# A third place for modulation weights, and the entry of the rotary attention in another order

## The reference, cut to what matters

```python
# first block, layer 1: keys and values from the norm with norm_kv, queries from norm_mix[1]
kv = _rmsnorm(h, norm_kv) @ w_kv
ks_ = _rope(ks_.reshape(b, s, N_HEADS, HEAD_DIM))
q = _rope((hn @ w_q_b[j]).reshape(b, s, N_HEADS, HEAD_DIM))
# _rope: [a1 * cos - a2 * sin, a2 * cos + a1 * sin]
...
# second block: w_ada_2 is 1024 x 6144
mod = jax.nn.silu(c) @ w_ada[l] + b_ada[l]
sh1, sc1, g1, sh2, sc2, g2 = jnp.split(mod[:, None, :], N_MOD, axis=-1)
u = rmsnorm(h, norm1_w[l]) * (1.0 + sc1) + sh1
```

## Time and profile before

| what | value |
|---|---|
| time, median of 3 runs | 1903.96 us (1902.36 to 1904.41) |
| the profiled execution's own time | 1905.59 us |
| its span in the trace | 1903.7 us |
| TensorE busy, granted clock over the span | 1854.5 us (97%), 0.993 |
| VectorE, ScalarE, GpSimd busy | 1302.0, 1036.9, 228.8 us |
| `down0` and the entry behind it | about 506 to 664 us of the span |
| `down1` | about 1111 to 1248 us of the span |

### The profile page before, as it was taken

The page is one execution under the profiler, slowest core; times in us unless marked ns, Lnnn a source line. Parts: engine busy times, 40 slices in busy tenths (PEclk is TensorE's granted clock), DMA queues, the critical chain, the costliest instruction groups (busy, mean ns, idle before and its releaser), DMA issues.

```text
span 1903.7 us, 29122 instructions
## 1 busy us (share of the span) xinstructions
PE 1854.5 (97%) x10924; PEld 1597.7 (84%) x10924; DVE 1302.0 (68%) x1962; ACT 1036.9 (54%) x1838; POOL 228.8 (12%) x239
## 2 busy tenths in 40 slices
PE   7999999999999899999999999999999999999997
PEld 6778788999888677778999987778888779999886
DVE  5566657888666767755888856598667687777322
ACT  5556545555577544445555557665556455555322
POOL 0000020111111100001111102211111101111000
PEclk9999999999999899999999999999999999999999
DMA  4211135666565322224566655532221135666431
GB/s 141 67 66 62 38 110 150 161 153 153 177 204 194 133 89 88 88 66 143 144 151 161 159 185 182 182 106 77 73 72 56 56 128 149 166 148 152 148 98 64
DMA packets 82452, 235.29 MB, mean 124 GB/s; under 512 B 10017, under 2 KB 10529, under 8 KB 81569
## 3 DMA queue, kind: packets, MB, share of 16 engines
q1 hardware_dynamic: 57984, 176.06, 27.9%
q0 software_dynamic: 23248, 56.11, 13.6%
q10 hardware_dynamic: 1104, 1.58, 0.2%
HBM read 221.12 MB, written 8.39 MB: 121 GB/s over the span
## 4 chain that ended last, share of the span: by engine, by line
PE 54%; DVE 5%; ACT 4%; DMA 3%; issue 2%; SPq 0%; POOL 0%; DVEq 0%; ACTq 0%; POOLq 0%
PE ps L413 9%; PE ps L415 9%; PE ps L414 9%; PE ps L1030 6%; PE ps L1031 6%; PE ps L1032 6%; PE ps L2825 2%; DMA wada<-in_ada 1%; PE ps L1636 1%; DMA tmps<-in_ada 1%; DVE wlo L395 1%; PE ps L1661 1%; PE ps L1651 1%; ACT wada L1488 1%; ACT tmps L1488 1%
## 5 line engine op out<-in xcount | busy, mean ns | idle before, releaser
L395 DVE TENSOR_TENSOR wlo<-raw,whi 128x1024 fp32r<-128x1024 f32 (+1 forms) x188 | 238.1, 1271 | 108.3 <-ACT whi L384 108.2
L413 PE MATMUL ps<-xh,whi 128*128 128x512 f32 x672 | 272.2, 405 | 6.3 <-DVE wlo L395 2.8
L414 PE MATMUL ps<-xl,whi 128*128 128x512 f32 x672 | 264.0, 393 | 0.0
L415 PE MATMUL ps<-xh,wlo 128*128 128x512 f32 x672 | 263.9, 393 | 0.0
L1031 PE MATMUL ps<-xl,whi 128*128 128x256 f32 x864 | 244.5, 283 | 0.0
L1030 PE MATMUL ps<-xh,whi 128*128 128x256 f32 x864 | 244.5, 283 | 0.0
L1032 PE MATMUL ps<-xh,wlo 128*128 128x256 f32 x864 | 244.4, 283 | 0.0
L384 ACT ACTIVATE whi<-raw 128x1024 fp32r<-128x1024 f32 (+1 forms) x196 | 197.9, 1023 | 76.2 <-PE ps L415 76.2
L413 PE MATMUL ps<-acth,whi 128*128 128x512 f32 x528 | 210.8, 399 | 8.8 <-DVE wlo L395 8.7
L784 ACT ACTIVATE whi<-raw 128x1024 fp32r<-128x1024 f32 x162 | 147.5, 911 | 112.5 <-PE ps L1032 99.1
L414 PE MATMUL ps<-actl,whi 128*128 128x512 f32 x528 | 206.0, 390 | 0.0
(11 more groups left out here) (382 smaller groups left out, 3770.1 us busy)
## 6 DMA issues: line engine op xcount, KB each, us to landing
raw<-in_gu SPq DMA_DIRECT2D x78, 512.0 KB, 3.8
raw<-in_down SPq DMA_DIRECT2D x48, 512.0 KB, 4.6
raw<-in_gu SPq DMA_DIRECT2D x54, 256.0 KB, 4.4
raw<-in_gu POOLq DMA_DIRECT2D x54, 256.0 KB, 4.5
raw<-in_qkv SPq DMA_DIRECT2D x24, 512.0 KB, 4.4
wada<-in_ada POOLq DMA_DIRECT2D x24, 512.0 KB, 3.8
tmps<-in_ada POOLq DMA_DIRECT2D x24, 512.0 KB, 3.9
raw<-in_qkvb SPq DMA_DIRECT2D x24, 512.0 KB, 3.8
```

What stands on the lines that cost most here:

```text
L395: eng.tensor_tensor(wlo[:, s, 0:n], raw[:, s, 0:n], whi[:, s, 0:n].bitcast(F32), ALU.subtract).then_inc(lo_done, 1)
L413: pe.matmul(ps[:, bank], whi[:, s, w], hi[:, k0 + k], start=start and k == 0, stop=False)
L414: pe.matmul(ps[:, bank], whi[:, s, w], lo[:, k0 + k], start=False, stop=False)
L415: mm = pe.matmul(ps[:, bank], wlo[:, s, w], hi[:, k0 + k], start=False, stop=stop and k == n - 1)
```

## The change

The fourth slot of `wlo` becomes a third place for units of `w_ada` in both down projections. The three places are used in turn, in an order that differs between the two phases, so that the last unit of the first phase lies in the new place, and the last in the second phase in the pair `tmps[:, 0:2]`. Three loads are issued at the start of a phase, and the load of unit n waits for the folding of unit n-3.

In the entry of the rotary attention, VectorE takes the query out of PSUM right behind the norm (ahead of the last four `yl`), splits the value unit directly behind the last `yl`, then takes the key out, splits the next query unit, multiplies both by `cosine`, and only then folds the last unit of `w_ada`. The two sign changes of `sine` go to ScalarE, behind a wait for the three tables and ahead of the two splits and two swaps that ScalarE makes there. TensorE makes the two last `ada_tile`s ahead of the last block of the value unit instead of between key and value unit. One semaphore is shared by two uses (`in_t`, `f_turned`) to make room for the third landing semaphore. Nothing else of the other stages changes.

```diff
+        third = top[0] + 3 * UNIT * 4
         wlo = place("wlo", [P, 4, UNIT], F32R)
...
-        ada_w = [wada[:, :], tmps[:, 0:2].rearrange("p a b -> p (a b)")]
+        ada_third = place("ada_third", [P, UNIT], F32, third)
+        ada_pair = tmps[:, 0:2].rearrange("p a b -> p (a b)")
+        ada_w = [(ada_pair, wada[:, :], ada_third[:, :]), (ada_third[:, :], wada[:, :], ada_pair)]
...
-                    wait(pool, ada_sum, n - 1)
-                    pool.dma_start(ada_w[n % 2], a["ada"][n, :, :]).then_inc(ada_in[n % 2], 16)
+                    wait(pool, ada_sum, n - 2)
+                    pool.dma_start(ada_w[n // 24][n % 3], a["ada"][n, :, :]).then_inc(ada_in[n % 3], 16)
...
-                load_ada(0, 2)
+                load_ada(0, 3)
...
-                    load_ada(3 * m + 2, 3 * m + 5)
+                    load_ada(3 * m + 3, 3 * m + 6)
...
-            par = j % 2
-            act.wait_ge(ada_in[par], t * 48 + 16 * ((24 * half + j) // 2 + 1))
+            par = j % 3
+            act.wait_ge(ada_in[par], t * 32 + 16 * ((24 * half + j) // 3 + 1))
...
                     split_hi(act, U["qkvb"], (0, 2))
+            act.wait_ge(at1.loaded, 48)
+            for part in (0, 64):
+                act.activation(sine[part:part + 32, :], sine[part:part + 32, :], ACT.Copy, scale=-1.0).then_inc(at1.signed, 1)
             u = U["qkvb"]
...
+            def query_first():
+
+                dve.wait_ge(mm_done, U["qkvb"].number(0, 0) + 1)
+                dve.scalar_tensor_tensor(tmp[0][:, :], ps[:, 6], 0.125, rstd[:, :], ALU.mult, ALU.mult)\
+                   .then_inc(at1.out, 1)
...
                 if m == 3:
                     refine_rest(dve, r0f)
-            ada_product(dve, 0, 3, 5)
-            dve.wait_ge(ada_sum, 24)
-            wait(dve, r0f.rstd, 4)
+                    wait(dve, r0f.rstd, 4)
+                    query_first()
+            split_lo(dve, U["qkvb"], (0, 2))
...
+            def rope_g(t):
                 if leading(t):
+                    key_out(t)
+                    split_lo(dve, u, ahead(u, t, 1, False))
+                    dve.wait_ge(at1.loaded, 48)
+                    query_cosined(t)
+                    key_cosined(t)
+                    ada_product(dve, 0, 3, 5)
+                    turn(t, 0, qrot)
                     ada_evac(dve, 0)
...
-                        if leading(t):
-                            for part_of in (4, 5):
-                                ada_tile(pe, 0, 3, part_of)
                     else:
                         pe.wait_ge(at1.out, 3 * t + 1)
-                        product(pe, u, t, 2, 6, yh, yl)
+                        product(pe, u, t, 2, 6, yh, yl, late=last_columns if leading(t) else None)
```

More of the change, by code:

```diff
@@ L442, in build @@
         e_lo = fast_prod = sem("e_lo_fast_prod")
-        in_t = sem("in_t")
+        in_t = sem("in_t_f_turned")
         out_in = sem("out_in")
-        f_ready, f_turned, f_moved = sem("f_ready"), sem("f_turned"), sem("f_moved")
+        f_ready, f_moved = sem("f_ready"), sem("f_moved")
+        f_turned = Since(in_t, KT)
         f_late, f_early = sem("f_late"), sem("f_early")
@@ L1118, in build @@
         hn = HeadNorm()
-        ada_in = [sem(f"ada_in{i}") for i in range(2)]
+        ada_in = [sem(f"ada_in{i}") for i in range(3)]
         ada_scaled = sem("ada_scaled")
@@ L1482, in ada_scale @@
         def ada_scale(act, half, t, j):
-            par = j % 2
-            act.wait_ge(ada_in[par], t * 48 + 16 * ((24 * half + j) // 2 + 1))
+            par = j % 3
+            act.wait_ge(ada_in[par], t * 32 + 16 * ((24 * half + j) // 3 + 1))
             for k in range(KT):
-                w = ada_w[par][:, k * P:(k + 1) * P]
+                w = ada_w[half][par][:, k * P:(k + 1) * P]
                 last = act.activation(w, w, ACT.Copy, scale=csil[:, k:k + 1])
@@ L1491, in ada_product @@
         def ada_product(dve, half, t, j):
-            n, par = t * 6 + (24 * half + j), j % 2
-            w = ada_w[par]
+            n = t * 6 + (24 * half + j)
+            w = ada_w[half][j % 3]
             dve.wait_ge(ada_scaled, n + 1)
@@ L2147, in _ @@
                     if m == 4:
-                        act.wait_ge(f_turned, 4)
+                        wait(act, f_turned, 4)
                         for b in range(NB):
@@ L2285, in turn, with query_cosined @@
                 dve.tensor_tensor(dst[:, :], dst[:, :], tmp[3 + i][:, :], ALU.add).then_inc(at1.roped, 1)
[L2287 to L2293, removed]
-                if leading(t):
[L2295 to L2300, removed]
+            def query_cosined(t):
@@ L2301, in rope_g, with key_out, key_cosined @@
                 dve.wait_ge(at1.out, 3 * t + 1)
                 dve.tensor_tensor(tmp[3][:, :], tmp[0][:, :], cosine, ALU.mult).then_inc(at1.cosined, 1)
-                split_lo(dve, u, ahead(u, t, 1, False))
+            def key_out(t):
                 dve.wait_ge(mm_done, u.number(t, 1) + 1)
                 dve.tensor_tensor(tmp[1][:, :], ps[:, 7], rstd[:, :], ALU.mult).then_inc(at1.out, 1)
+            def key_cosined(t):
                 dve.wait_ge(at1.out, 3 * t + 2)
                 dve.tensor_tensor(tmp[4][:, :], tmp[1][:, :], cosine, ALU.mult).then_inc(at1.cosined, 1)
+            def rope_g(t):
@@ L2308, in rope_g @@
                 if leading(t):
-                    ada_evac(dve, 0)
-                turn(t, 0, qrot)
-                if not leading(t):
+                    key_out(t)
[5 more added lines that the diff above has]
+                    turn(t, 0, qrot)
+                    ada_evac(dve, 0)
+                else:
+                    split_lo(dve, u, ahead(u, t, 0, False))
+                    dve.wait_ge(mm_done, u.number(t, 0) + 1)
+                    wait(dve, at1.roped, 2 * t)
+                    dve.scalar_tensor_tensor(tmp[0][:, :], ps[:, 6], 0.125, rstd[:, :], ALU.mult, ALU.mult)\
+                       .then_inc(at1.out, 1)
+                    query_cosined(t)
+                    split_lo(dve, u, ahead(u, t, 1, False))
+                    key_out(t)
+                    key_cosined(t)
+                    turn(t, 0, qrot)
@@ L2628, in _ @@
             wait(dve, f_rstd, 4)
-            dve.wait_ge(f_turned, KT)
+            wait(dve, f_turned, KT)
             for b in range(NB):
@@ L2737, in _, with last_columns @@
             u = U["qkvb"]
+            def last_columns():
+                for part_of in (4, 5):
+                    ada_tile(pe, 0, 3, part_of)
             def rope_g(t, part=(0, 1, 2)):
@@ L2981, in turn_rows @@
                     mm = pe.transpose(ps[:, 2 + b, m % 4 * P:(m % 4 + 1) * P], gain_h[:, m, b * P:(b + 1) * P], ident[:, :])
-                mm.then_inc(f_turned, 1)
+                mm.then_inc(f_turned.sem, 1)
             def sum_rows(squares, start):
```

1 line of the change is left out of this document (removed).

## The result

The changed kernel takes 1889.37 us, the median of 4 runs (1888.84 to 1890.44); the kernel before takes 1903.16 us, the median of 4 runs (1902.31 to 1904.41). The ratio is 0.9928, with a 95% interval of 0.9911 to 0.9945: 13.8 us shorter, within the range and next to the forecast of 1889.6. The sum behind the forecast was 14.4 us, counted from 1904.0; the fourth run of the kernel before brought its median down by 0.8 us, and so the time fits better than the gain. The profiled execution took 1888.85 us.

What follows compares the result with a forecast made beforehand. In `down1` late `w_ada` loads were taken to hold a 16.20 us round against TensorE's 15.70; 8.0 + 1.1 + 0.7 + 2.3 + 2.3 = 14.4 us off 1905.59, less 1.6 for the median, gave 1889.6 us, about 3 us either side.

Steps and rivals of the forecast that it cites:

- Part 1: Third place in `down1`: earlier loads remove TensorE's waits for low parts, 8.0 us, plus 1.1 us behind the last tile.
- Part 2: Third place in `down0`: 0.7 us within the tiles and 2.3 us at its end, ahead of the sum over partitions.
- Part 3: New order of the entry: scores start 2.3 us earlier, counted from S, the start of the sum over partitions.
- the clock's 0.94 us: Entry: with TensorE idle under 1 us before the sum over partitions, its clock stays and the norm's last step comes earlier.
- the 11.0 us from the value unit's low part to the scores: Entry: time from low part through SyncE's queue of loads and swaps to the scores, taken as 11.0 us before and after.
- rival (d): Scores: TensorE's idle time before them gets short enough for the clock to stay, 2.3 us less: 1887.3 us; chance 0.05.
- Rival (b): Entry gains nothing, key's swaps being late or TensorE waiting in the value unit: 2.3 us less gain, 1893 us; chance 0.12.
- (a): Another chain holds `down1`, tiles end at 16.4 us, half the gain there goes, 4 us: 1893.6 us; chance 0.12.
- (c): Waits put down to landings are really for SyncE's load or TensorE; only 2.3 us remain: 1901.7 us; chance 0.04.
- (e): Writes into the low parts' memory slow TensorE's reads in both down projections, 2.5 us per cent, 1910 at 8%; chance 0.02.
- six signs named: Landings, 0.75 us waits, 15.7 us tiles in `down1`; sum's wait under 1 us; value's low part at 8.4, scores 19.4 us.
- three signs of being wrong: `down1` rounds above 15.8 us without landings; sum over partitions waiting over 2 us; key's swaps landing later than 18 us after it.

Runs made afterwards that it cites:

- third_in_down1: The kernel before, with the third place and the earlier loads in `down1` alone: 1895.15 us, ratio 0.9959.
- order_alone: The changed kernel, three places still written in turn, but each load released by the folding of unit n-2 as before, so no lead: 1901.9 us, ratio 0.9996.
- third_alone: The changed kernel with the entry in its old order and the signs of `sine` on VectorE: 1891.3 us, ratio 0.9937; run again 1890.9 us, 0.9935.
- idle_filled: The changed kernel with 14 extra matmuls, sums unread, behind the value unit where TensorE idles ahead of the scores: 1887.95 us, ratio 0.9922.
- value_later: The changed kernel with swaps ahead of the unit's load, key turned before the value leaves PSUM, TensorE's wait for the value behind the scores: 1884.95 us, ratio 0.9913.
- sign_on_vector: The changed kernel with the two sign changes of `sine` back on VectorE, ahead of query times `cosine`: 1889.6 us, ratio 0.9932.

## Why the prediction was right, point by point

**Part 1, 8.0 and 1.1 us: right.** Tiles 2 to 7 give 103.56 - 95.91 = 7.65 us, and 0.4 more had been estimated for the tile before. Behind the last tile the first step that counts on (the twin sums' result on VectorE) comes 5.56 us after tile 7 instead of 6.7: 1.1 us. From one side of `down1` to the other it is 9.0 to 9.8 us in the two profiles of the changed kernel and that of `third_in_down1`, and 7.9 to 9.9 us over all with the lead.

**Part 2, 0.7 and 2.3 us: right, a little low.** From the first column sum of `down0` to S it is 118.5 to 119.0 us in the three profiles without the lead there and 115.3 to 115.4 in all those with it: 3.2 to 3.7 us.

**Part 3, 2.3 us: wrong.** Without the clock's 0.94 us the path was to give 1.4; the scores come 0.9 us (against the old order with the third place) to 1.3 us (`order_alone`) earlier behind S. Three steps failed. The first is the 0.94 us for the sum over partitions at full clock. It was put down to the wait ahead of S. But in `third_in_down1`, after 2.88 us of idle time, the sum took 1.12 us (the clock fell only behind it), and in `order_alone`, after 2.93 us, also 1.12 and the clock did not fall at all, against 1.80 in the profile of before. So where and whether the clock falls there differs between executions, and the size was too large as well: the norm's last step starts at S + 5.34 before and at S + 4.67 in `third_in_down1`, 0.67 us, and with the old order the scores start at S + 21.7 in both. The second is the 11.0 us from the value unit's low part to the scores, which were carried over from before: they were 11.6 us in the changed kernel and 11.8 in `order_alone`, because the query's swaps took 1.4 to 1.8 us longer from issue to landing and VectorE waited for them. The third is that the clock ahead of the scores was left as it was. The prediction had it as rival (d) in one direction only, for the new order, but it is the old order behind the third place that has the shorter idle time (2.4 us), and it pays for it with a fall of the clock in the value unit (7.3 us instead of 5.7). The new order runs that unit at full clock, idles 4.0 us and pays up to 1.7 us in the scores. Both need about the same to the transposes behind the scores: 24.3 and 24.0 against 23.5 and 24.6 us. Rival (b) describes what happened to this term: the order by itself gives 0.8 us (`order_alone`: 0.9996 of 1903.16, between 2.5 us shorter and 1.1 us longer), and nothing that shows beside the third place.

**Why the total came out all the same.** 9.1 and 3.2 to 3.7 us are 12.3 to 12.8 of the 13.8 measured; the two ratios of `third_alone`, which has no new order, agree with 12.0 and 12.4 us. About 1 us is left. It need not be the order's: from S to the step at 747.83 us before, the changed kernel is 2.6 and 2.7 us shorter than before, the kernel with the old order 1.8 and 3.4, and `third_in_down1`, unchanged there, 1.2. The comparisons can't divide it further. That the median hit the forecast within 0.3 us is luck: part 3 was too high, part 2 a little low, the median of the kernel before moved by 0.8 us, and the runs scatter by 1 to 2 us themselves.

**The rivals.** (a) fell: rounds of 14.4 us, TensorE last. (c) fell with the waits themselves, and `order_alone` brings them back. (e) fell: tiles take 15.70 us with DMA, ScalarE and VectorE writing into the third place. The Trainium skill's page SBUF — State Buffer, Who interferes with whom, says that TensorE waits on no one; the traces agree. (d) did not come with this change, since the idle time stayed at 4 us; with it shortened to 1.0 us in `idle_filled` and to 0.9 in `value_later`, it came: scores of 2.4 us, 2.2 less than before and 1.5 to 1.7 less than in the two profiles of the changed kernel.

**The signs.** Two instructions on ScalarE took 1.26 us (L1906 at 638.05), inside the bounds of 0.86 and 1.42. The Trainium skill's page ScalarE: Activation LUTs gave an estimated 1.13 us; the trace is 0.13 above. The move itself was worth nothing here (`sign_on_vector`), as VectorE waited for the swaps anyway, and 0.6 us of path once that wait was gone (one profile each).

**What would show it.** Of the six signs named, four came as said: landings, waits of 0.8 us, tiles, and the wait ahead of S. The low part was 0.3 us late, and the scores 0.85 us late. Of the three signs of being wrong one came, the key's last swap at S + 18.7 instead of 18 at most. It belongs to part 3, which did fail.

## What to carry to other kernels

One more buffer is worth the full length of the waits for a landing once the next limit of the round has been worked out (14.6 against 15.7 us here), and the check that it is the lead and not the buffer is to keep the buffer and release the loads as before. An order that brings the matrix engine's last work forward as much as the data leaves its idle time as it was (4.0 us here), and the price may come behind it, in the clock of the next work. So read an idle time together with the length of the work on both sides of it: the shorter one, 2.4 us, came with slower work ahead of it. In a queue that issues in order, put the short transfer that someone waits for ahead of the load that waits for a buffer.

## What the runs showed of the hardware

The granted clock after a short idle time of TensorE was not a function of its length alone. Ahead of the scores it stayed after 0.9, 1.0, 1.8, 2.2 and 2.4 us, fell after 2.15 and 2.42 us in two other profiles, and fell in all after 3.2 us or more (0.57 in the changed kernel; scores of 3.9 to 4.6 us instead of 2.4). Ahead of the value unit it stayed after 1.43 us (before) and 0.83 us (`third_in_down1`), and fell after 1.57 us in both profiles of the old order with the third place: about 1 us into the unit the products step 0.43 instead of 0.23 us. At the sum over partitions, with 2.9 us ahead of it in three profiles, it fell at the sum (before), right behind it (`third_in_down1`), and not at all (`order_alone`).

It also falls where TensorE does not idle. In the changed kernel 32 products with 2 columns each (L515) run from 1241.76 to 1245.38 us, and behind them the full products run at a lower clock for 3 us (two stretches):

```profile
1240.00:1246.00 6.00, 6.00 (x44) 5.58 (x43) 5.86 (x9) 2.90 (x4) 0.29 (x1) 1.00 0.22 87
1246.00:1250.00 4.00, 4.00 (x12) 3.11 (x11) 3.80 (x7) 2.17 (x3) 0.00 (x0) 0.57 0.00 0
```

Busy time of 4.00 in 4.00 us hides it; only the clock shows it. No run here tried to take this fall away.
